# Layer-norm gain moved behind a block-mixing product, its shift mixed by a product of its own, in a two-layer fp32 encoder trunk

## What is computed

```python
def spatial_gating_branch(u, v, z, ws, bs, ln_g, ln_b):
    v = layer_norm(v, ln_g, ln_b)          # over the 512 channels of a token; ends with y * g + b
    mask = chunk_id[None, :] <= chunk_id[:, None]
    w = jnp.where(mask[None], ws, 0)       # 4 groups of 128 x 128 weights over positions
    vb = v.reshape(b, s // 128, 128, 4, 128)
    mixed = jnp.einsum('gij,bnjgc->bnigc', w, vb) + bs.T[:, :, None]
    return u * mixed.reshape(b, s, 512) * jax.nn.silu(z)
```

## Time and profile before

| what | value |
|---|---|
| median of three runs | 778.59 us |
| the profiled execution's own time | 779.23 us |
| its span in the profile | 777.4 us |
| TensorE matmul (PE) busy | 769.0 us, 99% |
| VectorE (DVE) busy | 627.5 us, 81% |
| ScalarE (ACT) busy | 426.5 us, 55% |
| GpSimd (POOL) busy | 169.5 us, 22% |
| chain that ended last, by engine | PE 91%, DMA 3%, DVE 2%, issue 2%, ACT 1% |

### The profile page before, as it was taken

The page is one execution under the profiler, slowest core; times in us unless marked ns, Lnnn a source line. Parts: engine busy times, 40 slices in busy tenths (PEclk is TensorE's granted clock), DMA queues, the critical chain, the costliest instruction groups (busy, mean ns, idle before and its releaser), DMA issues.

```text
span 777.4 us, 12225 instructions
## 1 busy us (share of the span) xinstructions
PE 769.0 (99%) x4424; PEld 676.1 (87%) x4424; DVE 627.5 (81%) x1051; ACT 426.5 (55%) x790; POOL 169.5 (22%) x151
## 2 busy tenths in 40 slices
PE   7999999999999999999999999999999999999998
PEld 7988888888899889988899888888889998999887
DVE  5779999989778775779986799999887768746895
ACT  5566646442487447835564775652436773567242
POOL 1247511100230103012211674011012201110130
PEclk9999999999999999999999999999999999999999
DMA  9634237652796339585873522469138953577674
GB/s 333 228 100 144 83 105 141 165 133 82 138 160 194 83 79 163 179 237 116 188 244 90 183 82 82 125 146 216 56 83 167 184 164 63 111 141 223 169 145 127
DMA packets 54685, 113.67 MB, mean 146 GB/s; under 512 B 3552, under 2 KB 9120, under 8 KB 54624
## 3 DMA queue, kind: packets, MB, share of 16 engines
q0 software_dynamic: 22960, 47.27, 32.6%
q1 hardware_dynamic: 31376, 65.02, 26.3%
q10 hardware_dynamic: 288, 0.59, 0.2%
HBM read 97.14 MB, written 6.29 MB: 133 GB/s over the span
## 4 chain that ended last, share of the span: by engine, by line
PE 91%; DMA 3%; DVE 2%; issue 2%; ACT 1%; POOL 0%; SPq 0%; ACTq 0%; DVEq 0%; POOLq 0%
PE bank L868 17%; PE bank L866 17%; PE bank L867 17%; PE bank L946 7%; PE bank L948 7%; PE bank L947 7%; PE bank L999 5%; PE bank L840 2%; PE bank L858 2%; PE bank L915 2%; PE bank L917 2%; PE bank L916 2%; PE bank L796 1%; DMA x_sb<-in_x 1%; PE bank L849 1%
## 5 line engine op out<-in xcount | busy, mean ns | idle before, releaser
L1446 DVE TENSOR_TENSOR w_lo<-w_raw,w_hi 128x1024 fp32r<-128x1024 f32 x156 | 201.6, 1303 | 16.6 <-ACT w_hi L1084 10.7
L1084 ACT ACTIVATE w_hi<-w_raw 128x1024 fp32r<-128x1024 f32 x156 | 160.2, 1052 | 22.4 <-DMA w_raw<-in_w_out 15.9
L866 PE MATMUL bank<-w_lo,h_hi 128*128 128x512 f32 x256 | 100.5, 393 | 0.0
L868 PE MATMUL bank<-w_hi,h_hi 128*128 128x512 f32 x256 | 99.9, 390 | 0.0
L867 PE MATMUL bank<-w_hi,h_lo 128*128 128x512 f32 x256 | 99.8, 390 | 0.0
L740 POOL DMA_DIRECT2D w_raw<-in_w_in x32 | 38.6, 1207 | 227.4 <-DVE w_lo L1446 227.2
L946 PE MATMUL bank<-h_hi,w_lo 128*128 128x256 f32 x256 | 75.7, 296 | 0.0
L866 PE MATMUL bank<-h_lo,w_hi 128*128 128x512 f32 x192 | 75.2, 392 | 0.0
L868 PE MATMUL bank<-h_hi,w_hi 128*128 128x512 f32 x192 | 74.7, 389 | 0.0
L867 PE MATMUL bank<-h_hi,w_lo 128*128 128x512 f32 x192 | 74.7, 389 | 0.0
L948 PE MATMUL bank<-h_hi,w_hi 128*128 128x256 f32 x256 | 72.4, 283 | 0.0
(11 more groups left out here) (215 smaller groups left out, 1860.7 us busy)
## 6 DMA issues: line engine op xcount, KB each, us to landing
w_raw<-in_w_in SPq DMA_DIRECT2D x88, 512.0 KB, 4.3
w_raw<-in_w_in POOLq DMA_DIRECT2D x32, 512.0 KB, 6.0
w_raw<-in_w_out POOLq DMA_DIRECT2D x16, 512.0 KB, 6.6
w_raw<-in_w_out SPq DMA_DIRECT2D x12, 512.0 KB, 3.9
out<-x_sb POOLq DMA_DIRECT2D x4, 1024.0 KB, 5.5
w_raw<-in_w_oa SPq DMA_DIRECT2D x8, 512.0 KB, 3.5
w_raw<-in_w_ob SPq DMA_DIRECT2D x8, 512.0 KB, 4.0
x_sb<-out POOLq DMA_DIRECT2D x2, 2048.0 KB, 10.2
```

The lines of the kernel that those rows point to most:

```text
L866: nc.tensor.matmul(dst, s_h, m_l, start=(n == 0), stop=False)
L868: last = nc.tensor.matmul(dst, s_h, m_h, start=False, stop=(n == len(pairs) - 1))
L1084: nc.scalar.activation(hi, w_raw[:, raw_slot(layer, u)], ACT.Copy).then_inc(s_whi.sem, 1)
L1446: nc.vector.tensor_tensor(lo, w_raw[:, raw_slot(layer, u)], hi.bitcast(F32), ALU.subtract) \
```

## The change

The gain `a_ln_g` is no longer spread over the partitions. The host appends it to the gate's bias as four columns with channels on the partitions (`gate_raw` becomes 128x20), and `lng_bc` and its DMA go (`N_PARAMS` 5 to 4). `ln_apply` keeps its first instruction only. TensorE gets a new step, `mix_shift`, behind u's third job: four products of `lnb_bc` with the transposed mixing weights into bank 7. VectorE adds that bank to `bs_bc` at the end of what it does at n = `JOB_U[3]`. The bias add behind the mixing becomes a scalar_tensor_tensor: the mixed block times the gain's column, plus `bs_bc`.

```diff
-N_PARAMS = 5
+N_PARAMS = 4
+AFTER_SHIFT = JOB_U[2]
-            lng_bc = sb("lng_bc", [P, A_WIDTH], keep=early)
-        gate_raw = sb("gate_raw", [P, 2 * KD])
+        gate_raw = sb("gate_raw", [P, 2 * KD + A_GROUPS])
                 parameters = [
-                    (lng_bc, a_ln_g[l].to_broadcast([P, A_WIDTH])),
+            def mix_shift(layer):
+                pe.wait_ge(s_wsc.sem, s_wsc.at(layer, 1))
+                pe.wait_ge(s_wsz.sem, s_wsz.at(layer, 1))
+                pe.wait_ge(s_stage.sem, s_stage.at(layer, 3 * TILES))
+                for g in range(A_GROUPS):
+                    last = nc.tensor.matmul(bank[7][:, g * P:(g + 1) * P], lnb_bc[:, g * P:(g + 1) * P], ws_t[:, g],
+                                            start=True, stop=True)
+                last.then_inc(s_shift.sem, 1)
+                        if n == AFTER_SHIFT:
+                            mix_shift(layer)
             def ln_apply(layer, t):
                 tile = v_a[:, t]
-                vec.link(dve, nc.vector.tensor_scalar(tile, tile, mv[:, t, 0:1], ln_rstd[:, t:t + 1],
-                                                      ALU.subtract, ALU.mult))
-                vec.link(dve, nc.vector.tensor_tensor(tile, tile, lng_bc[:], ALU.mult))
-                nc.vector.tensor_tensor(tile, tile, lnb_bc[:], ALU.add).then_inc(s_ln.sem, 1)
+                nc.vector.tensor_scalar(tile, tile, mv[:, t, 0:1], ln_rstd[:, t:t + 1], ALU.subtract, ALU.mult) \
+                    .then_inc(s_ln.sem, 1)
-                    nc.vector.tensor_scalar(gate_half[:], gate_raw[:], 0.5, None, ALU.mult).then_inc(s_ghalf.sem, 1)
+                    nc.vector.tensor_scalar(gate_half[:], gate_raw[:, 0:2 * KD], 0.5, None, ALU.mult).then_inc(s_ghalf.sem, 1)
+                if n == AFTER_SHIFT + 1:
+                    dve.wait_ge(s_shift.sem, s_shift.at(layer, 1))
+                    vec.link(dve, nc.vector.tensor_tensor(bs_bc[:], bs_bc[:],
+                                                          bank[7][:].rearrange("p (g i) -> p g i", g=A_GROUPS), ALU.add))
-                    vec.link(dve, nc.vector.tensor_tensor(biased, m, bs_bc[:, g].unsqueeze(1).to_broadcast([P, TILES, P]),
-                                                          ALU.add))
+                    vec.link(dve, nc.vector.scalar_tensor_tensor(
+                        biased, m, gate_raw[:, 2 * KD + g:2 * KD + g + 1],
+                        bs_bc[:, g].unsqueeze(1).to_broadcast([P, TILES, P]), ALU.mult, ALU.add))
```

More of the change, by code:

```diff
@@ L245, in end_layer, with trunk @@
         self.n = self.waited = 0
-def trunk(nc, x, norm_g, w_in, gate_b, a_ln_g, a_ln_b, a_ws, a_bs, q_norm_g, k_norm_g, w_oa, w_ob, w_out,
+def trunk(nc, x, norm_g, w_in, gate_b, a_ln_b, a_ws, a_bs, q_norm_g, k_norm_g, w_oa, w_ob, w_out,
           ident, rope_cs, out):
@@ L406, in trunk @@
         s_mix = sig("mixed", A_GROUPS)
+        s_shift = sig("norm_shift_mixed", 1)
         s_um = sig("u_times_mixed", A_GROUPS)
@@ L769, in _ @@
         def _(pe):
-            seed(pe, s_job, s_xt, s_rott, s_idxp, s_wst, s_mix, s_qk, s_pt, s_pv)
+            seed(pe, s_job, s_xt, s_rott, s_idxp, s_wst, s_mix, s_shift, s_qk, s_pt, s_pv)
             def transpose_x(layer, t):
@@ L1863 @@
     gate = np.asarray(gate_b).reshape(DEPTH, 2, KD, P).transpose(0, 3, 1, 2).reshape(DEPTH, P, 2 * KD)
+    gate = np.concatenate([gate, np.asarray(a_ln_g).reshape(DEPTH, A_GROUPS, P).transpose(0, 2, 1)], axis=2)
     norm_g = np.broadcast_to(np.asarray(norm_g)[:, None, :], (DEPTH, P, D))
-    arrays = dict(x=np.asarray(x).reshape(SEQ, D), norm_g=norm_g, w_in=w_in, gate_b=gate, a_ln_g=a_ln_g,
+    arrays = dict(x=np.asarray(x).reshape(SEQ, D), norm_g=norm_g, w_in=w_in, gate_b=gate,
                   a_ln_b=a_ln_b, a_ws=a_ws, a_bs=np.asarray(a_bs).reshape(DEPTH, A_GROUPS * P), q_norm_g=q_norm_g,
```

## The result

The changed kernel takes 781.85 us in the median of seven runs (780.73 to 783.65), the kernel before 778.59 (778.21 to 779.26): a ratio of 1.0042, with a 95% interval of 1.0030 to 1.0053. It is slower by 3.26 us, and the interval goes from 2.3 to 4.1 us. The forecast was slower by 1.80, so the direction is right, the size is short by nearly half, and the median lies 0.25 us above the range's upper end of 781.6.

The account below looks back on a forecast made before the run. PE was taken to bound the kernel. Two layers of products at 0.90 us gave 1.80, all other terms 0: 778.59 + 1.80 = 780.4 us, slower by 0.23%, range 779.3 to 781.6.

Parts of the forecast that it names:

- The bound: Whole kernel: PE, busy 769.0 of 777.4 us, sets the time; only its work and its standing still can move it.
- The products' price: TensorE behind u's third job: four added fp32 products cost 0.90 us per layer, 1.80 in all.
- the lower rival (paced by columns): New products on TensorE: columns alone set the rate, 0.48 us per layer, 0.96 in all, 779.5 us; chance 0.06.
- the upper bound: New products on TensorE: eight records that do not overlap, 0.28 us each, 2.2 us per layer, 4.5 in all.
- The waits: `mix_shift` on TensorE: operands ready 20 us before, so its waits cost nothing.
- The bias add: VectorE behind the mixing: as scalar_tensor_tensor it still takes 0.69 us, so 0 change; up to 0.6 more each, hidden.
- The bound of 1.28 us: VectorE's bias add: worst case read from line 1504, taken as 512 columns of SBUF with a column scalar.
- Value 0; below nothing at most the PE idle of the crossover: VectorE's removed layer-norm instructions: relief worth 0 to the time, at most 0.19 us at the crossover between layers.
- The cover holds: VectorE's new add: 0.7 to 0.9 us fit in 1.9 us of room before the remainder, which waits for ScalarE.
- PE waits for none of it: Removed lines 1699 and 1700 on VectorE, 11.1 us: PE doesn't wait for them, so the value is 0.
- I see no row that prices it and take 0: SBUF tiles behind `gate_raw` shift by a few bytes: no profile row gives a cost, so 0.
- The range: Whole kernel: 779.3 to 781.6 us, from nearly the columns rival up to run spread and the stall's first part.

Follow-up runs that it names:

- the kernel before again: The kernel before, unaltered, run once more for a second trace: 778.38 against 778.60 us, ratio 0.9996.

## Why the prediction was half right

**The bound** was right. PE has 91% of the chain; VectorE relieved by 11 us alone gave nothing (1.0006), and every TensorE piece added or taken, 0.90, 1.80 or 0.5 us per layer, came through in the traces at its place. That VectorE's order of instructions can still hold PE is the step that failed, below.

**The products' price** was right: 0.90 forecast, 0.90 to 0.91 measured in all traces that have them, twice that when doubled. Both the lower rival (paced by columns) and the upper bound fell. The Trainium skill's 81 ns per matmul ("TensorE: Matmul & The Clock Gate", "Back-to-back issue gap") doesn't hold for these records; the traces have 112, in the mixing and in the new products alike (0.90 us for 8).

**The waits** of the new step were right: TensorE doesn't stop for it, and VectorE's add waits for nobody. It stood at 164.31 us, where 163.9 was forecast, with TensorE itself 0.35 late. The sum of PE's waits on VectorE was read short: the view has a third row, 0.4 us for `index_lo` at line 999, so it is 2.7 us and not 2.3; it sits at an index job too.

**The bias add** was put at 0.69 us and takes 0.751; it is hidden. The bound of 1.28 us beside it was misread: line 1504 has three shapes in the earlier trace rows, and 1.28 belongs to a 384-column instruction. The 512-column ones, with the scalar from a column, had the price before the run, 743 ns in the mean:

```profile
L1504 DVE SCALAR_TENSOR_TENSOR score<-probs,head_w,score 128x512 f32<-128x512 f32 x14 | 10.4, 743 | 0.4
```

**The step that failed is the one that put VectorE's changed stream at nothing for TensorE**: "Value 0; below nothing at most the PE idle of the crossover" for the removed instructions, and "The cover holds" for the new add. It priced what the instructions take, and not that all later ones move to other places in VectorE's stream. With the instructions removed and the add put in, one masked maximum starts 0.35 us later just where TensorE has no slack, and TensorE loses 0.30 us; without the add, or with one instruction more, it doesn't. Removal alone doesn't do it. The step rested on "PE waits for none of it", and those views don't show a stop of this size: the 0.30 us have no row among the waits and leave PE busy for 9.96 of 10.00 us. A second step, on the DMAs and places, "I see no row that prices it and take 0", missed 0.15 and about 0.13 us in the attentions, which come with the buffers' places. The steady sum is then 1.81 + 0.15 + 0.13 + 0.30 = 2.4 us.

**The range** was built on three runs that spread over 0.46 us. The kernel before spreads over 777.85 to 780.47 in 107 runs, 22 of them above 779.2, and the changed one over 780.54 to 783.65 in 17. The upper end left 1.2 us above the forecast; the steady pieces that the forecast lacks take 0.6 of it, and what differs between executions was given half a microsecond.

**Open** is about 0.6 us: the changed kernel measured +3.26, +2.9 and +3.1, and 2.4 are accounted for. Each of the three intervals takes in 2.4. All 17 executions together are 2.97 us over the 107 in the mean (95% about 2.5 to 3.4), which lies just above it, so something beyond the steady pieces is likely there. The ten at a granted clock of 1.000 are 2.7 above the kernel before, so that some 0.3 may go with the clock; more often fallen clocks are not shown. The start and crossover columns are large enough to hold the rest, which would need the changed kernel to meet the late values more often, and that is not shown either. Why the buffers' places slow the attention is open, and so is what happens near the multiples of 64 in VectorE's stream; no run tried a third set of places for the buffers.

## What to carry to other kernels

Where one engine is busy for the whole span, read what a change adds to that engine from the distance of two starts in rows of the same form, and expect little of relief elsewhere: here, trading 11 us of VectorE for 1.8 us of TensorE was a loss. Don't read from full busy windows that the engine never waits: a stop shorter than what the records overlap shows only as a longer step between two starts. For an effect of a fifth of a per cent, steady small terms of a tenth to three tenths of a microsecond came from places that no edit names (the stream of an engine without slack, buffer addresses), and one profiled execution may be half a microsecond or more off the median: take a second trace of the same kernel before sizing anything against it.

## What the runs showed of the hardware

- Three masked maxima on VectorE (10, 21, 29) start 0.35 or 0.71 us behind the instruction before, the same in every trace of one kernel, and otherwise when one instruction is added or left out far ahead of them. All 18 late starts stand within one record of a multiple of 64 in VectorE's stream.
- A scalar_tensor_tensor of 128x512 takes 0.75 us with a scalar from a column (0.751 at line 1736 with its source in PSUM, 0.752 at line 1679 in SBUF), and 0.69 with an immediate (line 1630 in the earlier trace rows).
- The granted clock fell for a few microseconds at the start in the changed kernel's first trace (0.57 from 24 to 28 us) and in the kernel before again (0.73 from 12 to 18). The first cost 1.26 us in its stretch, the second was made up by 25 us.
- A stop of TensorE of 0.30 us left PE's busy time at 9.96 of 10.00 us and no row among its waits.
- Taking away four transposes of 128 columns made TensorE 0.48 to 0.49 us earlier, against 0.44 read from the starts of the earlier trace rows.
